# Prompt scores of a hybrid decoder step: stacked split parts in block order, keys loaded a pair ahead, and a one-function root

## The reference

```python
xn = rmsnorm(x, norm_mix)
lru_x, lru_g, q, k, v = split(xn @ w_in)
xc = causal_conv(lru_x);  hs = rg_lru(xc)                 # a gated recurrence over time
y_lru = (hs * gelu(lru_g)) @ w_branch_lru
q = rmsnorm(q per head, q_gain); k = rmsnorm(k per head, k_gain)   # 24 heads of 64
for g, (window, dil) in enumerate(((128, 1), (512, 4), (2048, 16))):   # 8 heads each
    s = q . k / 8 + bias[distance], causal, inside the window, rows of one residue mod dil
    m = max(s); p = exp(s - m); l = sum(p); o = p v / l
o = merge of the three groups by l * exp(m - max m)
g_lru, g_att = split(sigmoid(xn @ w_merge + b_merge))
x = x + (g_lru * y_lru + g_att * (o @ w_branch_att)) @ w_o
x = x + swiglu_ffn(rmsnorm(x, norm_ffn))
```

## Time and profile before

| | |
|---|---|
| median of the runs | 2072.11 us |
| the profiled execution | 2071.17 us, its span 2069.4 us |
| PE busy | 2014.0 us, 97% |
| DVE, ACT, POOL busy | 905.9, 509.3, 552.1 us |
| moved by transfers | 188.45 MB, 91 GB/s on the mean |
| stages, us from the start | values to 75, recurrence to 300, queries and keys to 580, attention to 1041 |

### The profile page before, as it was taken

How to read it: one execution, slowest core, us unless ns; L and a number is a source line. 1 busy time by engine, 2 the same in 40 slices (tenths; PEclk the granted TensorE clock), 3 DMA queues, 4 the chain that set the end, 5 groups by cost and what they waited for, 6 DMA issues and landing times.

```text
span 2069.4 us, 32282 instructions
## 1 busy us (share of the span) xinstructions
PE 2014.0 (97%) x12884; PEld 1952.3 (94%) x12884; DVE 905.9 (44%) x919; ACT 509.3 (25%) x726; POOL 552.1 (27%) x325
## 2 busy tenths in 40 slices
PE   7999998999989999999989899999999999999999
PEld 7999997999979999999978899999999999999999
DVE  6666677777762332222266553433311233212331
ACT  5366653333333433333311111201000000000000
POOL 2323332222211111111122143323323232323322
PEclk9999999999999999999999999999999999999999
DMA  5211111222223323334286361111111111111112
GB/s 200 97 44 43 43 46 61 93 90 81 101 97 135 116 97 136 114 111 149 87 307 236 125 239 51 44 48 51 41 51 41 51 42 49 51 41 51 41 59 84
DMA packets 71595, 188.45 MB, mean 91 GB/s; under 512 B 9313, under 2 KB 28796, under 8 KB 70780
## 3 DMA queue, kind: packets, MB, share of 16 engines
q1 hardware_dynamic: 41456, 136.97, 19.5%
q10 hardware_dynamic: 30092, 50.81, 6.7%
HBM read 145.09 MB, written 45.81 MB: 92 GB/s over the span
## 4 chain that ended last, share of the span: by engine, by line
PE 89%; DVE 6%; ACT 1%; issue 1%; DMA 1%; POOL 0%; ACTq 0%; SPq 0%; DVEq 0%; POOLq 0%
PE ups L472 64%; PE ups L600 13%; PE ups L625 3%; PE ups L650 3%; PE aux L637 2%; DVE x L1335 1%; PE aux L538 1%; PE aux L559 1%; PE ups L486 1%; PE aux L614 0%; DVE x L1489 0%; DVE x L1259 0%; DMA x<-o_s 0%; DVE x L1280 0%; ACT x L1076 0%
## 5 line engine op out<-in xcount | busy, mean ns | idle before, releaser
L472 PE MATMUL ups<-big,wsp 128*128 128x344 f32 x9216 | 1477.3, 321 | 9.1 <-POOL wsp L450 6.6
L472 PEld LDWEIGHTS ups<-big,wsp 128*128 128x128 f32 x9216 | 1459.4, 189 | 24.0 <-issue 16.9
L448 POOL CAST wsp<-wraw 128x1024 fp32r<-128x1024 f32 (+2 forms) x160 | 167.8, 1049 | 1485.0 <-issue 724.0
L450 POOL TENSOR_TENSOR wsp<-wraw,wsp 128x1024 fp32r<-128x1024 f32 (+2 forms) x160 | 384.0, 2400 | 12.8
L600 PE MATMUL ups<-big,wsp 128*128 128x344 f32 x1728 | 291.8, 324 | 0.0
L600 PEld LDWEIGHTS ups<-big,wsp 128*128 128x128 f32 x1728 | 272.7, 189 | 5.3 <-issue 5.2
L1335 DVE RECIPROCAL x<-x 128x1024 f32<-128x1024 f32 x24 | 157.3, 6553 | 74.4 <-ACT x L1006 74.4
L1372 DVE SCALAR_TENSOR_TENSOR x<-ups,ext 128x256 f32<-128x256 f32 (+1 forms) x96 | 48.0, 542 | 235.4 <-PE aux L637 147.4
L1181 ACT ACTIVATE ext<-ext 128x1032 f32<-128x1032 f32 x22 | 23.6, 1071 | 482.5 <-DVE ext L1589 482.4
L1591 DVE TENSOR_TENSOR ext<-ups,ext 128x1032 f32<-128x1032 f32 x22 | 27.1, 1233 | 215.4 <-PE ups L472 215.4
L1605 DVE TENSOR_TENSOR x<-ups,x 128x1032 f32 x24 | 29.6, 1233 | 203.6 <-PE ups L472 203.6
(11 more groups left out here) (190 smaller groups left out, 1147.9 us busy)
## 6 DMA issues: line engine op xcount, KB each, us to landing
wraw<-w_in SPq DMA_DIRECT2D x52, 512.0 KB, 3.4
wraw<-w_ffn_in SPq DMA_DIRECT2D x44, 512.0 KB, 3.2
out_qkv<-x ACTq DMA_DIRECT2D x28, 512.0 KB, 2.7
ext<-out_qkv SPq DMA_DIRECT2D x24, 512.0 KB, 4.3
x<-x_T SPq DMA_DIRECT2D x16, 516.0 KB, 8.2
x<-gate_s SPq DMA_DIRECT2D x16, 516.0 KB, 4.1
wraw<-w_merge SPq DMA_DIRECT2D x16, 512.0 KB, 4.9
wraw<-w_ffn_out SPq DMA_DIRECT2D x16, 512.0 KB, 3.5
```

The lines of the kernel that those rows point to most:

```text
L448: nc.gpsimd.tensor_copy(hi, raw).then_inc(w_hi, 1)
L450: nc.gpsimd.tensor_tensor(lo, raw, hi.bitcast(F32), ALU.subtract).then_inc(w_split[slot], 1)
L472: ins = nc.tensor.matmul(ups[:, slot, c, 0:CH], wsp[:, slot, w, k, :], src[:, a, k, c * CH:(c + 1) * CH], start=(k == 0 and w + a == 0), s ...
```

## The change

1. Normed queries and keys are split once more: ACT writes a high part, DVE the low part, both in the block order of the group (`by_group`), so that the rows of a block lie side by side. SP stores them to a new scratch tensor `hs`, per head: the high part on partitions 0 to 63, the low part on 64 to 127 (`parts_store`, four transfers of 256 KB per tile).
2. The scores of a head and block are two fp32r matmuls of 128 partitions and always 256 keys: stacked queries with stacked keys (high by high plus low by low), and with the key parts exchanged (high by low plus low by high). Columns beyond the wanted keys are overwritten or not read. Two sets of key tiles alternate and are loaded a pair ahead (`key_loads`, six transfers, 2 MB); queries are loaded for both heads (1 MB) when the scores of the pair before are through. The pair loops are unrolled by two.
3. The root: ACT computes the reciprocal root by one function (`Abs_reciprocal_sqrt`), the 1/64 moves into the block of ones, and DVE makes one Newton step (three fused operations and a product in all, the gain multiplied by -0.5). The sums' buffer is free after the first of them (`nt_done`).
4. The recurrence's product is written once as float32 into `big2[:, 0]`; its high parts (ACT) and low parts (DVE) are made in the last pair of group 2.
5. Around the seams: the second tile of the query/key stage is copied out before the first root, low parts of squares are made ahead of or between the norms, and the loops of this stage on ACT, DVE and (in part) SP become straight code.

The diff's core (declarations and semaphores left out):

```diff
-QT, KTT, VT = ext[:, 2, 0:SEQ], ext[:, 3, 0:SEQ], tmp(2)[:, 0:SEQ]
+QH, QL = ([big2[:, 1, 4 + 2 * a + j, 0:SEQ] for j in range(2)] for a in range(2))
+QS, VT = [ext_r[:, 2 + h, 0:SEQ] for h in range(2)], tmp(2)[:, 0:SEQ]
+KS, KX = ([[big2[:, 1, 4 * n + 2 * a + h, 0:SEQ] for h in range(2)] for n in range(2)] for a in range(2))
+def by_group(ap, g):
+    d = (1, 4, 8)[g]
+    return ap.rearrange("p (d m) -> p m d", d=d)
+def key_window(ap, g, b):
+    c = (P * max(b - 1, 0), 256 * (b // 2), 256 * (b // 2))[g]
+    return ap[:, c:c + 256]
+def lru_part(a, k):
+    return big2[:, 1 - a, k, :]
...
-BT = ext[:, 0, 0:512].rearrange("p (h n) -> p h n", h=2)
+BT = tmp(6)[:, 512:1024].rearrange("p (h n) -> p h n", h=2)
...
         def query_loads(i, g):
-            for n, t in enumerate((QT, KTT)):
-                sp.dma_start(t, qkv_s[ds(i + (12 * n + 4 * g), 1)].rearrange("a p t -> p (a t)")).then_inc(qk_ld, 16)
+            for h in range(2):
+                sp.dma_start(QS[h].bitcast(F32), hs[ds(i + 4 * g, 1), h].rearrange("a p t -> p (a t)")).then_inc(qk_ld, 16)
+        def key_loads(i, g, n):
+            for h in range(2):
+                k = hs[ds(i + (12 + 4 * g), 1), h]
+                sp.dma_start(KS[n][h].bitcast(F32), k.rearrange("a p t -> p (a t)")).then_inc(key_ld[n], 16)
+                for a in range(2):
+                    sp.dma_start(KX[n][h][a * HD:(a + 1) * HD].bitcast(F32),
+                                 k[:, (1 - a) * HD:(2 - a) * HD].rearrange("a p t -> p (a t)")).then_inc(key_ld[n], 16)
...
+        def parts_store(i, j):
+            sp.wait_ge(ql_done[j], i + 1)
+            for h in range(2):
+                for a, t in enumerate((QH[j], QL[j])):
+                    sp.dma_start(hs[ds(i * 2 + j, 1), h, a * HD:(a + 1) * HD].rearrange("a p t -> p (a t)"),
+                                 t[h * HD:(h + 1) * HD].bitcast(F32)).then_inc(hs_stored[j], 16)
...
-            sp.wait_ge(qn_stored[0], 16 * 8)
-            query_loads(0, 0)
-            sp.wait_ge(qsl_done[0], 12)
+            for j in range(2):
+                parts_store(10, j)
+            sp.wait_ge(qn_done[0], 13)
             value_load(0, 0)
+            parts_store(11, 0)
             sp.wait_ge(bt_fill, 16)
-            sp.wait_ge(st_done[1], 13)
+            sp.wait_ge(qn_stored[0], 16 * 13)
             bias_load(0, 0)
+            parts_store(11, 1)
+            for j in range(2):
+                sp.wait_ge(hs_stored[j], 64 * 13)
+            key_loads(1, 0, 1)
...
+        if name == "qk":
+            def next_stores(i):
+                for slot in range(2):
+                    weights(i, slot)
+                for j in range(2):
+                    parts_store(i - 2, j)
+            with sp.Fori(2, 11) as i:
+                next_stores(i)
             for slot in range(2):
+                weights(11, slot)
+            for n in range(4):
+                sp.wait_ge(v_stored[n], 16)
+            sp.wait_ge(hs_stored[0], 64 * 8)
+            query_loads(0, 0)
+            key_loads(0, 0, 0)
+            for j in range(2):
+                parts_store(9, j)
+            continue
+        if name.startswith("att"):
+            g = int(name[3])
+            def next_loads(i, n, last=False):
+                for slot in range(2):
+                    weights(i, slot)
+                if g:
+                    for j in range(2):
                         sp.wait_ge(g_stored[j], 16 * (2 * g + 1))
                 sp.wait_ge(sa_done, 1)
                 sp.wait_ge(vt_mm, i + (4 * g + 1))
                 value_load(i, g)
+                sp.wait_ge(s_mm, i * 4 + 16 * g)
+                query_loads(i, g)
                 sp.wait_ge(sa_done, i * 4 + (16 * g + 1))
-                query_loads(i, g)
                 bias_load(i, g)
+                if not last:
+                    key_loads(i + 1, g, 1 - n)
+            if g == 0:
+                next_loads(1, 1)
+            with sp.Fori(int(g == 0), 2 - int(g == 2)) as ii:
+                for n in range(2):
+                    next_loads(ii * 2 + n, n)
+            if g == 2:
+                next_loads(2, 0)
+                next_loads(3, 1, True)
+            continue
...
         pe.wait_ge(qsl_done[j], i + 1)
-        pe.wait_ge(rt_done[1 - j], i + 1)
+        pe.wait_ge(nt_done[1 - j], i + 1)
...
     stats(0, 0)
     unit("qk", 1, 0, big1, parts=(1, 2))
-    unit("qk", 1, 1, big1, parts=(0,))
     stats(1, 0)
-    unit("qk", 1, 1, big1, parts=(1,))
+    unit("qk", 1, 1, big1, parts=(0, 1))
     stats(0, 1)
...
             pe.wait_ge(qk_ld, i * 48 + 48 * (4 * g + 1))
+            pe.wait_ge(key_ld[n2], (i - n2) * 48 + 96 * (2 * g + 1))
             for n in range(6):
                 if n < 4:
                     pe.wait_ge(sa_done, i * 4 + (16 * g + n + 1))
-                    for m in range(2):
+                    for m in ((1, 0) if g == 2 else (0, 1)):
                         b = 2 * n + m
-                        nk = nkeys(g, b)
+                        at = 128 if nkeys(g, b) == 1 and m == 0 else 256 * m
                         for hh in range(2):
-                            hr = slice(hh * HD, (hh + 1) * HD)
-                            ins = nc.tensor.matmul(s_bank[:, hh, 256 * m + 256 - P * nk:256 * m + 256], toks(QT, g, b)[hr],
-                                                   toks(KTT, g, b, nk)[hr], start=True, stop=True)
+                            for keys in (KS[n2][hh], KX[n2][hh]):
+                                ins = nc.tensor.matmul(s_bank[:, hh, at:at + 256], QS[hh][:, b * P:(b + 1) * P], key_window(keys, g, b),
+                                                       start=(keys is KS[n2][hh]), stop=(keys is KX[n2][hh]))
                     ins.then_inc(s_mm, 1)
...
-    pe.wait_ge(lru_done, KT)
+    pe.wait_ge(ul_done, KT)
...
-    def store(i, j):
+    def store(i, j, g=0):
         act.wait_ge(qn_done[j], i + 2)
+        act.wait_ge(hs_stored[j], i * 64 + 64)
+        nc.scalar.activation(by_group(QH[j], g), tmp(6 + j)[:, 0:SEQ].rearrange("p (m d) -> p m d", d=(1, 4, 8)[g]), ACT.Copy).then_inc(qh_done[j], 1)
         act.dma_start(qkv_s[ds(i * 2 + j, 1), :, :].rearrange("a p t -> p a t"), tmp(6 + j)[:, 0:SEQ]).then_inc(qn_stored[j], 16)
     def root(i, j):
         act.wait_ge(st_done[j], i + (1 + j))
         act.wait_ge(qn_done[j], i + 1)
-        nc.scalar.activation(tmp(4 + j)[:, 0:SEQ], aux[:].rearrange("p b n -> p (b n)"), ACT.Sqrt, scale=1.0 / HD, bias=epst[:])\
+        nc.scalar.activation(tmp(4 + j)[:, 0:SEQ], aux[:].rearrange("p b n -> p (b n)"), ACT.Abs_reciprocal_sqrt, bias=epst[:])\
             .then_inc(rt_done[j], 1)
     act.wait_ge(u_done, KT + 1)
     evac(0, 0)
+    act.wait_ge(z_done, KT + 1)
+    evac(0, 1)
     act.wait_ge(lru_done, KT)
+    root(0, 0)
...
-    root(0, 0)
-    evac(0, 1)
-    with act.Fori(1, 12) as i:
+    def next_pair(i, g):
         root(i - 1, 1)
         evac(i, 0)
-        store(i - 1, 0)
+        store(i - 1, 0, g)
         root(i, 0)
         evac(i, 1)
-        store(i - 1, 1)
+        store(i - 1, 1, g)
+    for i in range(1, 12):
+        next_pair(i, (i - 1) // 2 % NG)
+    store(11, 0, 2)
     root(11, 1)
-    store(11, 0)
-    store(11, 1)
+    store(11, 1, 2)
...
+                if last:
+                    act.wait_ge(s_mm, 44 + n)
+                    for k in range(n, KT if n == 4 else n + 1):
+                        nc.scalar.activation(lru_part(0, k), big2_f32[:, 0, k, :], ACT.Copy).then_inc(uh_done, 1)
...
-        step.step(nc.vector.tensor_tensor(U, H, GE, ALU.mult))
+        step.step(nc.vector.tensor_tensor(big2_f32[:, 0, ds(i, 1), :], H, GE, ALU.mult))
         dve.sem_inc(z_done, 1)
-        step.step(nc.vector.tensor_copy(big2[:, 0, ds(i, 1), :], U))
-        step.step(nc.vector.tensor_tensor(big2[:, 1, ds(i, 1), :], U, big2[:, 0, ds(i, 1), :].bitcast(F32), ALU.subtract))
         dve.sem_inc(lru_done, 1)
...
     def normed_qk(i, j):
-        rms_t = tmp(4 + j)[:, 0:SEQ]
+        y, t = tmp(4 + j)[:, 0:SEQ], tmp(2 + j)[:, 0:SEQ]
         dve.wait_ge(rt_done[j], i + (1 + j))
-        step.step(nc.vector.reciprocal(rms_t, rms_t))
+        step.step(nc.vector.scalar_tensor_tensor(t, aux[:].rearrange("p b n -> p (b n)"), EPS, y, ALU.add, ALU.mult))
+        dve.sem_inc(nt_done[j], 1)
+        step.step(nc.vector.tensor_tensor(t, t, y, ALU.mult))
+        step.step(nc.vector.scalar_tensor_tensor(t, t, -3.0, y, ALU.add, ALU.mult))
         dve.wait_ge(qn_stored[j], i * 16 + 16)
         nc.vector.scalar_tensor_tensor(tmp(6 + j)[:, 0:SEQ], tmp(j)[:, 0:SEQ], gqk[:, ds(i, 1)],
-                                       rms_t, ALU.mult, ALU.mult).then_inc(qn_done[j], 1)
+                                       t, ALU.mult, ALU.mult).then_inc(qn_done[j], 1)
+    def query_low(i, j, g=0):
+        dve.wait_ge(qh_done[j], i + 1)
+        nc.vector.tensor_tensor(by_group(QL[j], g), tmp(6 + j)[:, 0:SEQ].rearrange("p (m d) -> p m d", d=(1, 4, 8)[g]),
```

(78 more changed lines are left out.)

41 lines of the change are left out of this document (24 added, 17 removed).

## The result

The changed kernel took 2087.52 us (median of 10 runs, 2079.48 to 2096.73); the kernel before, beside it on the same chip, 2073.22 (median of 10 too; one of them took 8497.18). The ratio is 1.0071, 95% interval 1.0054 to 1.0088: slower by 0.7%, where 27.6 us (1.3%) less was forecast, and outside the range. The profiled execution took 2091.1 us, its span 2089.3.

A forecast was written before the change was run, and what follows sets the result against it. It took TensorE, busy 2014.0 of 2069.4 us, as the bound. Terms -16.0 (scores), -12.1 (seam 1), three of 0 and +0.5 (end of attention) gave -27.6: forecast 2044.5 us, range 2035 to 2060.

The forecast's parts named there:

- Attention: the loads: Attention, each pair's loads: they end at 339 GB/s as output stores begin; 0 us, from -1 to +16.
- the rule on shared queues: DMA engines take turns between queues with work, so a store beside a full queue gets about half.
- Rival (a): Attention: key loads collide with output stores, at 250 GB/s 8 pairs lose 2 us each: 2060 us; chance 0.12.
- rival (c): Attention scores: the split type falls to the float rate at 256 columns, +100 - 11.6, 2160 us; chance 0.07.
- 1.0 us of cover left: Group 1, step 0: margin between the exponential's end and its transposes, 2.4 us before the change.
- Attention: the scores: Attention: score matmuls at 120.7 ns, slots 0.966 us; groups 1 and 2 win 16.0 us, group 0 wins 0.
- the exponential's wait: Group 0: PE already waits 1.0 us for ACT's exponential before transposes, so the 1.5 us gain there counts 0.
- Seam 1: Recurrence to queries and keys: standing 9.5 and low clock 2.6 us at the sums vanish, -12.1 us.
- the working on DVE's chain: Seam 1: three fused steps and a product take 5.1 us against 7.8, freeing the sums buffer after the first.
- Seam 2: Query/key stage into attention: earlier low parts offset by values and bias behind part stores; 0, from -6 to +5 us.
- End of attention: After the last pair: the recurrence's split delays PE 1.9 us, the sample's preparation costs +0.5, from 0 to +2 us.
- steady part: Query/key stage: units stay 12.26 us of PE, slower block-order writes stay hidden; 0, up to +5 us.

The follow-up runs named there:

- e7: Changed kernel with each head's exchanged key tile loaded by one whole 128-partition load of unexchanged keys, not two of 64 partitions (cross products left out): 2041.88 us, ratio 0.9843.
- e11: Changed kernel with each exchanged key tile loaded by two loads of 128 partitions and half the columns, keys unexchanged (cross products left out): 2046.93 us, ratio 0.9869.
- e12: Changed kernel with keys asked for one pair later, without waiting for the landed store, and values and bias ahead of three part stores: 2038.01 us, ratio 0.9830.
- e8: e2 with the root undone: square root and reciprocal in place of the one-function root and its Newton step: 2050.98 us, ratio 0.9889.
- e2: e1 plus values and bias asked for ahead of three of the last four part stores at the start of attention: 2038.82 us, ratio 0.9838.
- e1: Changed kernel with keys asked for one pair later, behind the values and after the output store two pairs back has landed: 2047.60 us, ratio 0.9871.
- e13: Changed kernel with key parts stored three times, whole key loads at the change's place, and values and bias ahead of three part stores: 2051.50 us, ratio 0.9895.

## Why the prediction was wrong

**The step that failed** is in "Attention: the loads": 3.75 MB "at 339 GB/s" are through when the store leaves, "They touch and hardly overlap", 0. The rate was the mean of a queue whose large loads in the kernel before filled all 128 partitions. Four of the six new key loads, with half the bytes, fill 64, and with them the engines moved about 205 GB/s, so the store landed in 8.9 us instead of 3.8. With whole-width loads (e7, e11) the sentence holds: in e11 the burst ends just before the store leaves, and groups 1 and 2 win 18.5 us. The Trainium skill has the rule (SBUF — State Buffer, "Door 1: The DMA port swizzle"): partitions 0 to 63 reach only 8 of the 16 ports through which DMA writes, so a tile of 64 partitions gets 196 GB/s at 1 MiB, and about 218 at most. The trace agrees on the rate, about 205 against 300 to 430 GB/s, for loads of 256 KB; the ports themselves no run shows. The same page of the Trainium skill ("Can I just issue two DMAs to hit both halves?") says that two loads for both halves at one time gain 6% over one. The trace does not contradict it: the two halves of a tile were asked for within 1.2 us on one queue, and the rate stayed at about 205; whether both moved at one time is not shown. The prediction had weighed the rule on shared queues and not the one on the shape, which the diff shows.

**Rival (a)** was the right wait, at the right place, with too small a chance (0.12) and price (+16); the cause, the narrow loads, it did not have. Its rate of 250 GB/s gave a store 3 us late; it was 5 (8.9 against 3.8), and later at the worst. It counted 2 us a pair; PE stood 24.0 us in 6 places and 5.9 more for ACT. And it had no term for the clock, 17 us. So it ended at 2060, still faster than before: the chance of 0.07 for slower was rival (c)'s alone, and no branch of the forecast had a slower kernel by this wait. Its "about half" for a store beside a full queue is not what the trace shows either: 0.02 MB beside 0.79 from 780 to 784 us. The prediction had itself the two signs: 1.0 us of cover left, and the falling clock at both seams after waits of this size.

**Attention: the scores.** The mechanism was right, the size a little small. 118 ns a matmul (0.94 / 8; I took 120.7, the line through both widths gave 118). Groups 1 and 2: -18.5 in e12 against -16.0; group 0: -3.0 in the change against 0, so the exponential's wait did not eat it. At 118 ns the slots themselves give 16.7 and 1.9 of that; where the rest comes from is not shown.

**Seam 1.** -10.6 against -12.1. The rows of the changed kernel that answer to the earlier trace rows:

```profile
306.13 1.09 PE L640 MATMUL aux<-ext_r,bones_r 128*128 128x512 f32 x4
...
314.62 1.09 PE L640 MATMUL aux<-ext_r,bones_r 128*128 128x512 f32 x4
...
323.50 1.15 PE L640 MATMUL aux<-ext_r,bones_r 128*128 128x512 f32 x4 [0.24 <-DVEq L1436]
...
336.76 1.19 PE L640 MATMUL aux<-ext_r,bones_r 128*128 128x512 f32 x4 [0.78 <-DVE ext_r L1372]
```

From first to last 30.6 us, where it was 41.3 and 29.2 was worked out; of the rest, 1.0 us are the two short waits. By e8 the root is needed for it, as the working on DVE's chain had said.

**Seam 2.** +6.5 against 0, just outside -6 to +5. The step "values and bias now stand behind two part stores" was right; its landing at 339 GB/s was not: the 2.75 MB took 15 us, from 583.1 to 598.1, where 10 to 12 were worked out, and began 24.7 us after the last unit's start instead of 22.0. The part stores are narrow too, 64 partitions each, and from 584 to 590 us they and the values moved at 206 GB/s with the engines 0.95 busy. Whether this is the cause at the seam as well was not tried. The timeline of the changed kernel there:

```profile
587.40 4.19 SPq L416 DMA_DIRECT2D hs<-big  x4
591.69 2.00 SPq L410 DMA_DIRECT2D x<-bt_s  x1
...
598.15 2.08 PE L707 MATMUL ups<-big,ext_r 128*128 128x256 f32 x8 [3.48 <-DMA x<-bt_s]
```

The bias is issued behind the first part store of unit 11, and the scores come 6.5 later. With the bias ahead of it (e2, e12) the 6 us go.

**End of attention, steady part.** The wait before the branch product is 2.9 us (up to 2.7 forecast), and the stretch behind it is 4.3 shorter, mostly a wait of 4.5 us in the sample part that vanished: not foreseen, by +0.5. It is not shown to be the change's: the same wait is back in e1 (4.6) and e13 (4.5), whose sample part is the same. The steady units kept 12.26 us, as forecast, although the writes in block order were slower, as had been allowed for.

**The sum.** Forecast -27.6. With the seam as forecast and loads that do not hurt (e12) the spans differ by -36.9; with the change's seam and whole-width loads (e11) by -27.0. That this is the forecast's -27.6 is partly luck: seam 2 costs 5.8 there, and group 0 (-2.5), groups 1 and 2 (2.5 more than forecast) and the end (-1.2) make it good. The rate of 339 GB/s for narrow transfers was the error that decided.

## What to carry to other kernels

Before pricing a transfer by a rate from the trace, compare its shape with the transfers that made that rate: partitions filled, bytes per row. A DMA share near 1.0 says nothing of the rate; read it beside the GB/s. Where a small store stands between one tile's work and the next, ask what is in flight when it leaves, how many us of cover its reader has, and what the clock costs after the cover is gone: here 17 us on 28 of waits, 60% on top.

## What was not expected of the hardware

- Key loads half of whose bytes fill 64 partitions: all engines busy (0.98 of 769 to 782 us), at about 205 GB/s from 775 to 784.5, against 280 to 430 in 128 partitions with the same number of loads.
- A 264 KB store beside them landed in 8.9 us, in the kernel before in 3.8, and in 4.6 where copies inside DRAM ran at their place. Its queue moved 0.02 MB from 780 to 784 us, while the narrow loads ran on the other queue, and 0.95 in the next 4.
- Six waits of 4 us on the mean and some short ones, 28 us in 317, cost 17 us more by the clock.
- Eight stacked score matmuls of 256 columns took 0.94 us, 118 ns each, with weight loads of 188 ns (median) hidden.
- Writing a tile in the block order of groups 1 and 2 (elements 4 or 8 apart) took 2.08 us on ACT and 2.02 on DVE; in group 0, where they lie side by side, 1.04 and 1.22.
